# Attention of the second layer on one Trainium2 core: value products of two heads as two 64-column tiles

## The reference, cut to what matters

```
o_cmp, p_cmp = compressed_attention(q, k_cmp, v_cmp, slopes)      # 31 compressed keys
o_slc = selected_attention(q, ks, vs, p_cmp, slopes)              # 8 of 8 blocks of 64 keys: causal attention
o_win, _ = banded_attention(q, kw, vw, slopes, WIN_SIZE - 1, 1)   # window of 512: causal attention
o = gates[..., 0:1] * o_cmp + gates[..., 1:2] * o_slc + gates[..., 2:3] * o_win
y = concat([o * silu(z), ym * silu(zm)])
```

## Time and profile before

| what | us |
|---|---|
| kernel before, median of 3 runs | 3182.96 |
| lowest and highest of these | 3180.08, 3183.6 |
| the profiled execution, its span | 3192.1 |
| PE busy in it | 3015.6 (94%) |
| DVE busy in it | 1910.3 (60%) |
| this stage in the trace, from its first scores to its last finish | 806.2 to 990.4 |

### The profile page before, as it was taken

The page is one execution under the profiler, slowest core; times in us unless marked ns, Lnnn a source line. Parts: engine busy times, 40 slices in busy tenths (PEclk is TensorE's granted clock), DMA queues, the critical chain, the costliest instruction groups (busy, mean ns, idle before and its releaser), DMA issues. The chain is left out here.

```text
span 3192.1 us, 35825 instructions
## 1 busy us (share of the span) xinstructions
PE 3015.6 (94%) x13812; PEld 2381.4 (75%) x13812; DVE 1910.3 (60%) x2848; ACT 1137.8 (36%) x1969; POOL 344.8 (11%) x476
## 2 busy tenths in 40 slices
PE   7989999899999899999999899999999999989997
PEld 6768867777776686776787678868677678767885
DVE  5743335462675545755645688864575564568887
ACT  3441131321444112153002577731215300157774
POOL 0120020000442001210000200010121000011001
PEclk9999999999899999999999999999999999999999
DMA  3213302233701232202234699933220232469995
GB/s 127 86 60 93 93 22 80 65 109 112 303 1 64 70 119 64 85 14 67 92 93 164 257 374 403 392 106 119 64 85 14 66 92 93 172 252 351 406 404 195
DMA packets 155504, 465.19 MB, mean 146 GB/s; under 512 B 17190, under 2 KB 34760, under 8 KB 129992
## 3 DMA queue, kind: packets, MB, share of 16 engines
q1 hardware_dynamic: 146552, 430.94, 37.8%
q0 software_dynamic: 8784, 31.99, 2.6%
HBM read 413.08 MB, written 49.81 MB: 145 GB/s over the span
## 5 line engine op out<-in xcount | busy, mean ns | idle before, releaser
L167 DVE CAST weights_r<-weights 128x1024 fp32r<-128x1024 f32 (+4 forms) x248 | 206.0, 831 | 644.2 <-DMA weights<-in_w_in 210.1
L169 DVE TENSOR_TENSOR weights_r<-weights,weights_r 128x1024 fp32r<-128x1024 f32 (+4 forms) x248 | 361.4, 1457 | 8.5
L154 PE MATMUL ps<-x_cols_hi_r,weights_r 128*128 128x512 f32 x896 | 361.4, 403 | 4.4 <-DVE weights_r L355 2.9
L155 PE MATMUL ps<-x_cols_lo_r,weights_r 128*128 128x512 f32 x896 | 357.2, 399 | 0.0
L156 PE MATMUL ps<-x_cols_hi_r,weights_r 128*128 128x512 f32 x896 | 356.9, 398 | 0.0
L1101 POOL TENSOR_SCALAR weights<-weights,weight 128x256 f32<-128x256 f32 (+3 forms) x304 | 152.5, 523 | 670.7 <-DVE weight L995 407.7
L1045 ACT ACTIVATE weights<-weights,minus_top 128x256 f32<-128x256 f32 (+3 forms) x304 | 166.8, 550 | 119.3 <-DVE minus_top L958 119.2
L154 PEld LDWEIGHTS ps<-x_cols_hi_r,weights_r 128*128 128x128 f32 x896 | 170.5, 190 | 50.9 <-issue 4.6
L155 PEld LDWEIGHTS ps<-x_cols_lo_r,weights_r 128*128 128x128 f32 x896 | 170.5, 190 | 42.0 <-issue 1.4
L156 PEld LDWEIGHTS ps<-x_cols_hi_r,weights_r 128*128 128x128 f32 x896 | 170.2, 190 | 41.7
L154 PE MATMUL ps<-hawk_xT_hi_r,weights_r 128*128 128x512 f32 x384 | 154.0, 401 | 6.6 <-DVE weights_r L169 5.4
(11 more groups left out here) (577 smaller groups left out, 6937.9 us busy)
## 6 DMA issues: line engine op xcount, KB each, us to landing
weights<-in_w_in SPq DMA_DIRECT2D x76, 512.0 KB, 4.1
weights<-in_hawk_w_in SPq DMA_DIRECT2D x52, 512.0 KB, 3.9
weights<-in_w_in SPq DMA_DIRECT2D x26, 1024.0 KB, 5.3
x_cols_hi<-in_w_exp_gate SPq DMA_DIRECT2D x22, 1024.0 KB, 7.4
x_cols_lo<-in_w_exp_up SPq DMA_DIRECT2D x18, 1024.0 KB, 8.8
attn_T<-in_w_exp_down SPq DMA_DIRECT2D x18, 1024.0 KB, 8.5
weights<-in_w_exp_down SPq DMA_DIRECT2D x16, 1024.0 KB, 8.3
block_x<-expert_x_rows SPq DMA_DIRECT2D x31, 512.0 KB, 8.8
```

The costliest lines, as they stand in the source:

```text
L154: pe.matmul(out, as_r(left[1]), as_r(right[0]), start=start, stop=False)
L155: pe.matmul(out, as_r(left[0]), as_r(right[1]), start=False, stop=False)
L167: dve.tensor_copy(as_r(hi), lo).then_inc(rounded, 1)
L169: dve.tensor_tensor(as_r(lo), lo, as_r(hi).bitcast(F32), ALU.subtract).then_inc(done, 1)
```

## The change

In the stage of the second layer only:

- **Two tiles.** The stationary block is now 64 columns wide (`v_[:, j, g, 64:128]`, the values alone). The even head's products go to PSUM partitions 0 to 63, the odd head's to 64 to 127; in the built program they carry a tile size of 128x64 and the positions 0 and 64 in the array's columns. The matmuls of the two heads are issued in turns: even j = 0, odd j = 0, even j = 1, and so on. The compressed product stays full width.
- **Units paired.** The order of the table units in a quad is now head h0 selected, h0 + 1 selected, h0 window, h0 + 1 window. The product step stands only with the odd head's unit, and does both heads of that branch.
- **Four key buffers** (`n_keys=4`) in place of two, since a product reads two of them; a copy waits for the product that read the buffer four units ago (`keys_left`). The two more lie in new tiles `more_scores`.
- **Four table rows** in place of two, with the wait four heads back.

```diff
@@ column_attention
-        places_ = [room[b // 3][:, (b % 3) * width:(b % 3 + 1) * width] for b in range(min(6, n_buf + 2))]
-        for _ in range(n_buf + 2 - 6):
+        places_ = [room[b // 3][:, (b % 3) * width:(b % 3 + 1) * width] for b in range(min(6, n_buf + n_keys))]
+        for _ in range(n_buf + n_keys - 6):
             places_.append(sb("more_scores", [P, width])[:, :])
...
-            return by_key[k % 2][:, c["dst"]:c["dst"] + c["n"]]
+            return by_key[k % n_keys][:, c["dst"]:c["dst"] + c["n"]]
+
+        def keys_left(k):
+            old = k - n_keys
+            if old < 0:
+                return 0
+            return cnt.products[old + (1 if units[old].get("products") is not None or not units[old]["chunks"] else 2)]
...
-                products = u["products"](by_key[k % 2], cmp_keys)
-                for n, (left, right, col, n_cols) in enumerate(products):
-                    mm = pe.matmul(ps[:, out + col:out + col + n_cols], left, right, start=u["first"] and n == 0,
-                                   stop=bool(u.get("finish")) and n == len(products) - 1)
+                if u.get("paired"):
+                    products = u["products"](by_key[(k - 1) % n_keys], by_key[k % n_keys], cmp_keys)
+                else:
+                    products = [(slice(0, P), *p) for p in u["products"](by_key[k % n_keys], cmp_keys)]
+                for n, (to, left, right, col, n_cols) in enumerate(products):
+                    mm = pe.matmul(ps[to, out + col:out + col + n_cols], left, right, start=u["first"] and n == 0,
+                                   stop=bool(u.get("finish")) and n >= len(products) - (2 if u.get("paired") else 1))
                 mm.then_inc(s.multiplied, 1)
@@ copy on DVE, and the same on ACT
-                        if k >= 2 and cnt.products[k - 1]:
-                            dve.wait_ge(s.multiplied, cnt.products[k - 1])
+                        if keys_left(k):
+                            dve.wait_ge(s.multiplied, keys_left(k))
@@ nsa_attention
-        rows = sb("table_rows", [P, 2, SEQ])
+        rows = sb("table_rows", [P, 4, SEQ])
...
-            for h in range(4 * q, 4 * q + 4):
+            for h0 in (4 * q, 4 * q + 2):
                 for b, (k_, v_) in enumerate(((ks, vs), (kw, vw))):
-                    first, last = h % 2 == 0 and b == 0, h % 2 == 1 and b == 1
-
-                    def products(keys, cmp_keys, h=h, v_=v_, g=g, q=q, first=first):
-                        cmp = [(v_cmp[:, g, (h % 4) // 2, :], cmp_keys[:, q % 2, :], 0, SEQ)] if first else []
-                        at = 64 if h % 2 == 0 else 0
-                        return cmp + causal_products(keys, lambda j: v_[:, j, g, at:at + P])
+                    def products(even_keys, odd_keys, cmp_keys, h0=h0, b=b, v_=v_, g=g, q=q):
+                        cmp = [] if b else [(slice(0, P), v_cmp[:, g, (h0 % 4) // 2, :], cmp_keys[:, q % 2, :], 0, SEQ)]
+                        sides = [[(slice(64 * i, 64 * i + 64), *p) for p in causal_products(keys, lambda j: v_[:, j, g, 64:128])]
+                                 for i, keys in enumerate((even_keys, odd_keys))]
+                        return cmp + [p for both in zip(*sides) for p in both]
...
-        column_attention(nc, m, units, 1, 3, 4, 4, "alone", tables, zero_rows=(moe.x_rows, moe.y_rows), zeros=zeros, idle=(6, 4, 4, 2))
+        column_attention(nc, m, units, 1, 3, 4, 4, "alone", tables, zero_rows=(moe.x_rows, moe.y_rows), zeros=zeros, idle=(6, 4, 4, 2), n_keys=4)
```

More of the change, by code:

```diff
@@ L799, in column_attention @@
 def column_attention(nc, m, units, n_sets, lag, n_buf, n_slots, mode, tables=None, finish_by="dve", minus_lam=None,
-                     zero_rows=(), zeros=None, loads=(), idle=(), early=()):
+                     zero_rows=(), zeros=None, loads=(), idle=(), early=(), n_keys=2):
     ps = m.ps
@@ L1062, in copy @@
                         act.wait_ge(s.turned, cnt.chunks[k] + n + 1)
-                        if k >= 2 and cnt.products[k - 1]:
-                            act.wait_ge(s.multiplied, cnt.products[k - 1])
+                        if keys_left(k):
+                            act.wait_ge(s.multiplied, keys_left(k))
                         act.activation(key_place(k, c), ps[:, c["at"]:c["at"] + c["n"]], ACT.Copy).then_inc(s.copied_act, 1)
@@ L1082, in build @@
             def build(head):
-                if head >= 2:
+                if head >= tables.get("n_rows", 2):
                     pool.wait_ge(s.scanned, tables["free"](head, cnt))
@@ new lines, in nsa_attention @@
+                    for h in (h0, h0 + 1):
+                        unit_of[h, b] = len(units)
+                        more = dict(products=products, paired=True, out=6 + (h // 2) % 2, first=b == 0,
+                                    finish=(lambda dve, bank, n=h // 2: gated_by(yT)(dve, bank, n)) if b else None) if h > h0 else {}
+                        units.append(unit(
+                            "table", head=h, opens=b == 0, gate=gates[:, :, 3 * h + b + 1],
+                            tables=causal_tables(rows[:, h % 4, :]),
+                            pieces=causal_pieces(m, lambda out, t, h=h, k_=k_: stacked_scores(out, qs[:, h, t * P:(t + 1) * P],
+                                                                                              k_[:, g, :, 0:(t + 1) * P])),
+                            chunks=causal_chunks(1536), **more))
@@ L1866, in nsa_attention @@
         slopes = alibi_slopes(NSA_HEADS)
         def build(pool, head):
-            return pool.tensor_scalar(rows[:, head % 2, :], causal[:, :], -slopes[head], 1.0, ALU.mult, ALU.mult)
+            return pool.tensor_scalar(rows[:, head % 4, :], causal[:, :], -slopes[head], 1.0, ALU.mult, ALU.mult)
         def build_quad(pool, q):
@@ L1874, in build_quad @@
             return ins
-        tables = dict(n=NSA_HEADS, build=build, build_quad=build_quad, free=lambda head, cnt: cnt.pieces[unit_of[head - 2, 1] + 1],
+        tables = dict(n=NSA_HEADS, build=build, build_quad=build_quad, n_rows=4, free=lambda head, cnt: cnt.pieces[unit_of[head - 4, 1] + 1],
                       free_quad=lambda q, cnt: cnt.pieces[unit_of["cmp", q - 2] + 1])
-        column_attention(nc, m, units, 1, 3, 4, 4, "alone", tables, zero_rows=(moe.x_rows, moe.y_rows), zeros=zeros, idle=(6, 4, 4, 2))
+        column_attention(nc, m, units, 1, 3, 4, 4, "alone", tables, zero_rows=(moe.x_rows, moe.y_rows), zeros=zeros, idle=(6, 4, 4, 2), n_keys=4)
 def tables_rider(sb, m, a):
```

## The result

The changed kernel takes 3169.48 us, the median of 9 runs (3165.4 to 3181.64), against 3183.6 (3180.08 to 3200.42) of the kernel before beside it. The ratio of the runs is 0.9943 with a 95% interval of 0.9926 to 0.996, so it is 0.4% to 0.7% faster. In a second set of executions the ratio was 0.9958 (0.9943 to 0.9972). The forecast was 3174.8, in a range of 3163 to 3198. As a difference the forecast was 8.2 us, and the two medians differ by 14.1.

The account below looks back on a forecast made before the run. The prediction took PE to bound the stage, with DVE 1.2 us a unit behind. Each quad falls from 42.55 to 40.5 us, 2.05 less, 8.2 for four: 3182.96 - 8.2 = 3174.8 us, range 3163 to 3198.

Parts of the forecast that it names:

- P: PE's time from a pair's eight matmuls to the next scores, without compressed product: taken as 2.9 us, bounds 2.28 to 4.36.
- the second compressed product: Compressed product in a quad's rounds: the forecast counted it once, at 0.86 us, in round 7.
- rival C: In the pair's products: full overlap of the tiles, P = 2.3 us, 18 us off, 3165 us; chance 17%.
- What bounds the stage: In the changed stage: PE, busy 182.9 of 186 us; what it saves should come off the whole kernel.
- The list of rounds: A quad's nine rounds, from scores start to scores start: sum 28.9 + 4 P, 40.5 us against today's 42.55.
- round 7: In a quad: a pair's round with the compressed product of 0.86 us, 3.57 + P.
- round 2: In a quad, after the compressed scores: scores, turn wait, turns and the pair's products, 2.71 + P.
- Rounds without a product: In each quad: PE waits for DVE's tops, 2.81 us a round, or DVE's own 3.35 for the second in a row.
- The clock: PE's granted clock in the stage: up to three more falls from new gaps, 1.64 us each, 5 us into the range.
- Start and end: First and last parts of the stage: go the same way as the quads; each pair at the end still saves 1.26 us.
- Rival A: In the pair's products: tiles don't overlap, P = 4.36 us, 15 us slower, 3198 us; chance 20%.
- Rival D: In the pair's products: loads never beside the other tile's pass, P = 6.6 us, 51 us slower, 3234; chance 3%.

Follow-up runs that it names:

- e2_wide: Changed kernel's order, pairs, four key buffers and table rows, but each product full width with half the stationary block zeros; stage 200.0 us, whole kernel 3200.70 us.
- e1_blocks: Changed kernel with a pair's products issued as the even head's four, then the odd head's four, not in turns; stage 194.6 us, whole kernel 3203.39 us.
- e7_twos: Changed kernel with a pair's products issued in turns of two matmuls per head; a pair took 2.35 us, stage 173.0 us, whole kernel 3182.84 us.
- e3_alone: Kernel before, same order and two buffers, but each head's product 64 columns wide in its own tile, one head at a time; stage 193.1 us, whole kernel 3199.30.
- e4_fill: Changed kernel with six idle products after the turns in the rounds of the second to fourth compressed unit; stage 167.8 us, whole kernel 3168.94 us.
- e8_repeat: Changed kernel with each compressed score streaming its 32 key columns four times (128 columns); stage 162.8 us, whole kernel 3169.22 us.
- e5_split: Changed kernel with the compressed product one unit earlier and each pair's middle key tiles moved to the next round; stage 160.5 us, whole kernel 3165.33 us.
- e9_both: Changed kernel with products spread over rounds as in e5_split and compressed scores streaming 128 columns; stage 153.8 us, whole kernel 3160.13 us.
- e10_old_repeat: Kernel before with only the compressed scores streaming 128 columns; stage 179.3 us, whole kernel 3189.58 us.

## Why the prediction was right, and where it was off

The direction, the time (5.3 us over the median) and the range held. That the time came so near is in part luck: the two largest errors, P and the second compressed product, have opposite signs. The case that came is not the one behind the forecast (3172 to 3178, 40%) but rival C (3161 to 3170, 17%), which the range took in. Two of the signs of being wrong were just missed: P is 2.31 and had to be over 2.3, and the granted clock of the stage is 0.93 and was not to fall below it. By its steps:

- **What bounds the stage.** Right: PE's product time came off one for one (16 x 1.93 = 30.9 us by pairs, 31.1 by the stages of e2_wide and the changed kernel). DVE's busy time went only from 122.6 to 121.4 us. What the stage gained is in the span, and nothing after it took it back.
- **P, taken as 2.9.** Too large: 2.31, the lower end of the bounds (2.28) and rival C. The step that failed here is "if matmuls start in order, the first even pass (0.43) runs alone". It does not, since a pass of the free tile goes past up to three waiting passes of the busy one (e1_blocks, e7_twos). The 0.2 for late loads wasn't there either: loads also come in twos. That is 0.59 x 16 = 9.4 us. On the other hand two changes of tiling cost 0.31 with what they add to the turns, not 0.20 (e3_alone).
- **The second compressed product.** The list of rounds has it once in a quad, in round 7; it stands also with the second pair of heads, in round 2. With it, and 0.95 instead of 0.86 for each, the sum is 29.9 + 4 P, 39.2 with the P that came out; e4_fill's quad without a fall took 39.14. It cost some 4 us of the forecast's gain, in error the other way than P.
- **Rounds without a product.** Right, to the hundredth: 2.81, and 3.13 where I had 3.35. Only in the third quad one of them takes 3.06 to 3.09, in all eight traces in which it stands, with pauses in DVE's scan whose cause stays open. That these rounds are what the change pays is shown by e2_wide (+15.8 us with nothing but the order) and by filling them: 8.4 us off with e5_split, and 9.0 from e8_repeat to e9_both, where no clock falls behind later units.
- **The clock.** It was foreseen as up to three more falls of 1.64 us, against a base that I took from a quad without one. By the table of the stage's parts, the changed kernel's three falls behind compressed units cost 5.6 us against e8_repeat (1.86, 1.87 and 1.85), and the start 0.6; but the kernel before had two falls, which cost 5.0 us against e10_old_repeat (3.37 and 1.64). The net is 0.6 us for these falls. I had put the risk on PE's new gaps; e8_repeat has the same gaps and no fall behind a later unit, so what decided there was how many columns the compressed scores stream, with the two limits said at that run. Why a fall cost 3.37 us in one place and 1.64 in another, and why the kernel before escaped behind one of its three later units, stays open.
- **Start and end.** By quads the corrected sum is 4 x (42.55 - 39.2) = 13.4 us; without falls behind later units the stage gained 179.29 - 162.77 = 16.5. Of the rest, 3.1, some 2.1 is in the last part (5.5 against 3.4), where the drain was not worked out, and 0.6 in the first, where e10_old_repeat ran at the low clock for a time and e8_repeat didn't.

The finish stayed hidden: in the third quad it runs from 899.93 for 0.69 us, and the scan starts at 900.82, 1.01 after the scores (899.81), as in a round without it (1.03 at 892.32). For waits on key buffers or table rows there is no room: the corrected sum of a quad has none, and is 39.2 where 39.14 was measured.

Rival A needed tiles that don't overlap: its price was about right (e2_wide's pairs at 4.24 for its 4.36, and e1_blocks part of the way), its condition was not met. Rival D, loads in the open, did not happen: a load of 64 columns of one tile runs under the other's pass. The Trainium skill, "TensorE: Matmul & The Clock Gate", Part 3, says that matmuls start and end strictly in program order and that a load overlaps running matmuls only where the row groups differ. The order of starts does not hold between two column tiles here (840.42 ahead of 840.63 and 840.95, e1_blocks), nor does the rule on loads (two loads at 840.41, one for each tile, while passes run); the measurement decides. Its figure for three column tiles (2.38 times, from which the prediction estimated 0.79 of the full gain for two) was low for these: 4.24 to 2.31 is 1.84 times, or 0.92.

## What to carry to other kernels

Two 64-column tiles worked off in turns did twice the work in the time of one here (2.31 us against 2.30), in fp32, but only where the instructions of the two tiles stood within a few of each other: three waiting passes were passed, four not. Whatever is brought together for it leaves rounds in which the bound engine waits for the next one in the ring; count those rounds as a cost (here half of what the tiles brought), and spread the work again where buffers allow it. Look at what stands before a fall of the clock: here it was mostly 32 scores of 32 columns each, and streaming 128 columns under the same loads cost no time and went with no fall behind the later units, though at the first it helped in one trace of three at most.

## What the runs showed of the hardware that I had not expected

- Passes of two column tiles start 0.01 us apart, and a pass goes ahead of three waiting ones of the other tile (e1_blocks, e7_twos), but not of four (e1_blocks at 840.09).
- A product in a 64-column tile alone costs 0.31 us more than at full width, 0.22 in its own step and 0.09 in that of the turns before it (e3_alone).
- The granted clock fell to half in every run whose compressed scores streamed 32 columns, behind two or three of the three later units (25 of 30 in ten traces), and behind none of nine where they streamed 128 (e8_repeat, e9_both, e10_old_repeat), at equal time of the scores. Around the first unit it was low in all traces but that of e8_repeat, whatever they streamed.
- A fall costs more where the rounds behind it are full: 1.9 us in the changed kernel, 3.1 in the first round behind e5_split's fourth unit.
